# LayerNorm of the convolution: from the compress and prompt stages into the decode passes, with its channel sums added on VectorE

## The reference, cut to what matters

```python
def conformer_conv(u, buf, w, b, ln_g, ln_b):
    xx = jnp.concatenate([buf, u], 1)
    y = dwconv_valid(xx, w) + b
    y = jax.nn.silu(layer_norm(y, ln_g, ln_b))
    return y, xx[:, -(CONV_WIDTH - 1):]

def merge_and_ffn(...):
    c, conv_state = conformer_conv(u, ...)
    x = x + jnp.concatenate([o_nsa, c], -1) @ w_out
    ...
```

## Time and profile before

| what | value |
|---|---|
| median of 3 runs | 1894.15 us (1892.86 to 1899.56) |
| the profiled execution | 1898.77 us, span 1897.0 us |
| mean granted TensorE clock | 0.997 |
| busy share of the span | TensorE 98%, VectorE 66%, ScalarE 20%, GpSimd 6% |
| layer 0: compress, prompt, decode | from about 178, 221 and 308 us of the span |
| layer 0: output projection, layer 1 | from about 452 us; layer 1 follows some 935 us behind layer 0 |

### The profile page before, as it was taken

One profiled execution on the slowest core, in us unless ns is written; L12 is line 12 of the kernel. 1 busy time (PEld: TensorE's weight loads), 2 busy tenths in 40 slices (PEclk: granted clock), 3 DMA queues, 4 the chain that ended last, 5 costly groups with the idle time before them and its releaser, 6 DMA issues.

```text
span 1897.0 us, 26865 instructions
## 1 busy us (share of the span) xinstructions
PE 1855.6 (98%) x10198; PEld 1414.7 (75%) x10198; DVE 1253.0 (66%) x2636; ACT 371.6 (20%) x957; POOL 118.4 (6%) x219
## 2 busy tenths in 40 slices
PE   8999999999999999999999999998999999999999
PEld 7767677777777777777777676776777777777777
DVE  5899896453666766673268998944536667676631
ACT  2013474322100000100001125832221000000000
POOL 1011400010000000000000113000000000000000
PEclk9999999999999999999999999999999999999999
DMA  7303563673121212131241044057531121222211
GB/s 282 127 1 89 157 204 127 205 241 109 63 67 67 89 67 89 58 133 62 85 161 59 1 141 121 2 179 233 168 109 56 67 89 67 89 67 87 93 61 50
DMA packets 110851, 200.28 MB, mean 106 GB/s; under 512 B 13793, under 2 KB 81650, under 8 KB 105730
## 3 DMA queue, kind: packets, MB, share of 16 engines
q1 hardware_dynamic: 105154, 168.17, 26.6%
q0 software_dynamic: 5568, 30.39, 4.6%
HBM read 190.82 MB, written 15.94 MB: 109 GB/s over the span
## 4 chain that ended last, share of the span: by engine, by line
PE 71%; DVE 20%; SPq 5%; issue 2%; ACT 1%; DMA 1%; POOL 0%; DVEq 0%
PE ps L1048 30%; PE ps L1113 15%; DVE catT L1598 7%; PE ps L612 7%; PE ps L599 5%; PE ps L748 4%; SPq L363 2%; PE ps L851 2%; PE ps L814 2%; PE ps L833 2%; SPq L345 1%; PE ps L899 1%; DVE catT L1605 1%; PE ps L984 1%; DVE rC L1604 1%
## 5 line engine op out<-in xcount | busy, mean ns | idle before, releaser
L1598 DVE SCALAR_TENSOR_TENSOR catT<-XC,par,catT 128x512 f32<-128x512 f32 x240 | 180.3, 751 | 7.5
L2097 DVE TENSOR_TENSOR xT<-xT,ps 128x288 f32<-128x288 f32 (+3 forms) x55 | 41.7, 758 | 153.2 <-PE ps L1113 152.9
L1048 PE MATMUL ps<-catT,rD 128*128 128x288 f32 x528 | 131.6, 406 | 0.0
L1048 PEld LDWEIGHTS ps<-catT,rD 128*128 128x128 f32 x528 | 100.3, 190 | 27.7
L1048 PE MATMUL ps<-catT,XC 128*128 128x288 f32 x480 | 119.8, 406 | 0.4 <-DVE rD L2011 0.4
L748 PE MATMUL ps<-WR,rD 128*128 128x254 f32 (+1 forms) x512 | 119.2, 382 | 0.2
L1463 ACT ACTIVATE rD<-rD 128x592 f32<-128x592 f32 x44 | 30.7, 697 | 450.2 <-DVE rD L2039 450.2
L1048 PE MATMUL ps<-rA,WR 128*128 128x288 f32 x448 | 117.8, 406 | 0.0
L1048 PEld LDWEIGHTS ps<-catT,XC 128*128 128x128 f32 x480 | 91.0, 190 | 26.2 <-issue 1.2
L748 PEld LDWEIGHTS ps<-WR,rD 128*128 128x128 f32 x512 | 93.3, 187 | 18.7 <-issue 2.9
L1048 PEld LDWEIGHTS ps<-rA,WR 128*128 128x128 f32 x448 | 85.1, 190 | 23.5
(11 more groups left out here) (371 smaller groups left out, 3341.8 us busy)
## 6 DMA issues: line engine op xcount, KB each, us to landing
WR<-in_w_up SPq DMA_DIRECT2D x56, 512.0 KB, 3.8
WR<-in_kvc SPq DMA_DIRECT2D x128, 128.0 KB, 2.4
rB<-in_ksT SPq DMA_DIRECT2D x256, 64.0 KB
rB<-in_w_up SPq DMA_DIRECT2D x32, 512.0 KB, 4.4
rD<-in_kvc SPq DMA_DIRECT2D x96, 128.0 KB
rD<-in_w_down SPq DMA_DIRECT2D x8, 1408.0 KB, 7.7
rB<-in_w_down SPq DMA_DIRECT2D x6, 1408.0 KB, 6.2
WR<-in_w_glu SPq DMA_DIRECT2D x16, 512.0 KB, 3.7
```

The costliest lines, as they stand in the source:

```text
L1048: ins = mm(ps[:, bank, 0:HN], w[:, k, :], h[:, k, :], start=k == 0, stop=k == 3)
L1598: ins = stt(yc[:, 0:SEQ], xc[:, k:k + SEQ], w, yc[:, 0:SEQ], ALU.mult, ALU.add)
L2097: step(tt(x, x, src, ALU.add))
```

## The change

The sum over channels is split: VectorE adds the four tiles (`ln_add`), then TensorE multiplies one tile of sums by ones (`conv_sum`, 2 matmuls in place of 8), and the same for the squares (`ln_squares`, `conv_sum`). The mean is taken at the prompt's end (`ln_centre`), the squares' sum and variance at p = 0, the inverse root at p = 1 (`root`, `ln_root`), scaling at p = 1 and 2, and the gates of tiles 0 to 2 at p = 2 and of tile 3 at p = 3. `hidden(l, 2, 3, 1)` is redistributed: ten of its steps go to where `means` stood, three and three into the prompt. Two helper tiles `lnu`, `lnv` lie in the convolution's input tile XC, so the load of the next layer's history there (L415) moves to the decode's end.

```diff
@@ -203,9 +203,7 @@
 o += 2 * NT
-lnsq = [rA[:, 576 * i:576 * (i + 1)] for i in range(2)]
-lnmu = rA[:, 1152:1728]
-lnrs = [rA[:, 4192:4192 + HN], rB[:, 5120:5120 + HN]]
+lnu, lnv = [XC[:, 2 * i:2 * i + 2, XS0:XS0 + HN] for i in range(2)]
@@ -411,8 +409,6 @@
         sp.wait_ge(*count("uc_out", 16))
-        if l + 1 < DEPTH:
-            sp.dma_start(XC[:, :, XS0:XW], I["hist"][l + 1].rearrange("p (c n) -> p c n", c=CT)).then_inc(sh["hist_in"], 16)
@@ -442,6 +438,9 @@
                 fetch_new(l, p + 2)
+        sp.wait_ge(sh["conv_done"], CT * (l + 1))
+        if l + 1 < DEPTH:
+            sp.dma_start(XC[:, :, XS0:XW], I["hist"][l + 1].rearrange("p (c n) -> p c n", c=CT)).then_inc(sh["hist_in"], 16)
@@ -656,14 +655,6 @@
-    def means(l):
-        pe.wait_ge(sh["tr_kept"], 10 * l + 10)
-        for c in range(CT):
-            pe.wait_ge(*count("conv_made"))
-            for hf in range(2):
-                ins = mm(ps[:, 2 + hf, 0:HN], ones[:, :], catT[:, CT + c, hf * HN:(hf + 1) * HN], start=c == 0, stop=c == CT - 1)
-        ins.then_inc(sh["mu_made"], 1)
@@ -726,7 +717,7 @@
             for i in range(2):
-                ins = tr(ps[:, (5, 7)[t // 2], (2 * (t % 2) + i) * P:(2 * (t % 2) + i + 1) * P],
+                ins = tr(ps[:, (5, 4)[t // 2], (2 * (t % 2) + i) * P:(2 * (t % 2) + i + 1) * P],
@@ -784,15 +775,19 @@
         keys_second(l, 1, NCP, prompt_pick, CG[0])
-        means(l)
+        hidden(l, 2, 3, 1, js=range(10))
...
         prompt_values()
-        for c in range(CT):
-            square_sum(c, 2, lnsq, CT)
         keys_T(NCS)
+    def conv_sum():
+        pe.wait_ge(*count("u_ready"))
+        for hf in range(2):
+            ins = mm(ps[:, 1 + 2 * hf, 0:HN], ones[:, :], lnu[:, hf, :], start=True, stop=True)
+        ins.then_inc(sh["u_summed"], 1)
@@ -855,12 +850,11 @@
         pe.wait_ge(*count("cs_max"))
-        pe.wait_ge(sh["var_made"], 6 * l + 4)
         scores(0)
+        hidden(l, 2, 3, 1, js=range(10, 13))
+        scores(1)
+        hidden(l, 2, 3, 1, js=range(13, 16))
         pe.wait_ge(sh["cmp_in"], 16 * l + 5)
-        hidden(l, 2, 3, 1, js=range(8), bank=4)
-        scores(1)
-        hidden(l, 2, 3, 1, js=range(8, 16), bank=4)
@@ -872,8 +866,9 @@
             turn(v)
+        pe.wait_ge(*count("masked"))
+        conv_sum()
         weigh(15)
-        pe.wait_ge(*count("masked"))
@@ -890,6 +885,8 @@
             pe.wait_ge(*count("ks_in", 512))
+            if p == 0:
+                pe.wait_ge(*count("u_read", 2))
@@ -966,13 +963,14 @@
                 else:
-                    pe.wait_ge(*count("conv_done", 3))
...
                 pe.wait_ge(*count("st_kept", 2))
+                if p == 0:
+                    conv_sum()
@@ -1006,11 +1004,14 @@
             if more:
+                if p == 0:
+                    pe.wait_ge(*count("u_read", 2))
...
                 else:
+                    pe.wait_ge(*count("conv_done", 3))
@@ -1269,10 +1270,6 @@
-    def ln_square(c):
-        act.wait_ge(*count("mu_taken"))
-        square(c, lnsq, catT[:, CT + c, :])
@@ -1323,17 +1320,12 @@
         copy(KcT[4][HD:P, 32:32 + NCP], ps[HD:P, 6, P:P + NCP]).then_inc(sh["kct_kept"], 1)
-        ln_square(0)
-        ln_square(1)
...
         ins.then_inc(sh["vct_kept"], 1)
-        ln_square(2)
-        ln_square(3)
-        act.wait_ge(*count("sq_summed", 2))
@@ -1366,12 +1358,10 @@
         exps(0)
-        root(lnrs[0])
-        root(lnrs[1])
...
         for i in range(2):
-            copy(CT8[:, 4 * i:4 * i + 4, :], ps[:, (5, 7)[i], :].rearrange("p (k n) -> p k n", n=P)).then_inc(sh["ct_kept"], 1)
+            copy(CT8[:, 4 * i:4 * i + 4, :], ps[:, (5, 4)[i], :].rearrange("p (k n) -> p k n", n=P)).then_inc(sh["ct_kept"], 1)
@@ -1393,17 +1383,17 @@
             act.activation(S[:, 2056:2576], S[:, 2056:2576], ACT.Exp, bias=st[:, 15:16], scale=SCALE, accum_out=st[:, 17:18]).then_inc(sh["w_exped"], 1)
-            if p == 0:
-                act.wait_ge(*count("ln_made", 4))
-            else:
-                act.wait_ge(*count("conv_done"))
-            act.activation(thl, catT[:, CT + p, :], ACT.Tanh, scale=0.5).then_inc(sh["ln_tanh"], 1)
+            if not more:
+                act.wait_ge(*count("conv_done", 3))
+                act.activation(thl, catT[:, CT + p, :], ACT.Tanh, scale=0.5).then_inc(sh["ln_tanh"], 1)
...
                 tanhed(tanh[0], NCS)
+            if p == 1:
+                root(lnv)
@@ -1421,6 +1411,10 @@
                 values_kept(NCS, Vc[ba % 4], 2)
+                if p == 2:
+                    act.wait_ge(*count("ln_made", 4))
+                    for c in range(3):
+                        act.activation((halves(thl), lnu, lnv)[c], halves(catT[:, CT + c, :]), ACT.Tanh, scale=0.5).then_inc(sh["ln_tanh"], 1)
@@ -1685,27 +1679,53 @@
+    def ln_add(l):
+        dve.wait_ge(sh["uc_out"], 16 * (l + 1))
+        y = [halves(catT[:, CT + c, :]) for c in range(CT)]
+        tt(lnu, y[0], y[1], ALU.add)
+        step(tt(lnv, y[2], y[3], ALU.add))
+        tt(lnu, lnu, lnv, ALU.add).then_inc(sh["u_ready"], 1)
+    def ln_summed(bias):
+        dve.wait_ge(*count("u_summed"))
+        for hf in range(2):
+            ts(lnv[:, hf], ps[:, 1 + 2 * hf, 0:HN], 1.0 / CC, bias, ALU.mult, ALU.add).then_inc(sh["u_read"], 1)
+        dve.wait_ge(*count("u_read", 2))
     def ln_centre():
-        dve.wait_ge(*count("mu_made"))
-        step(ts(halves(lnmu), ps[:, 2:4, 0:HN], 1.0 / CC, None, ALU.mult))
+        ln_summed(0.0)
         for c in range(CT):
-            tt(catT[:, CT + c, :], catT[:, CT + c, :], lnmu, ALU.subtract).then_inc(sh["mu_taken"], 1)
+            y = halves(catT[:, CT + c, :])
+            ins = tt(y, y, lnv, ALU.subtract)
+        step(ins)
+    def ln_squares():
+        y = [halves(catT[:, CT + c, :]) for c in range(CT)]
+        tt(lnu, y[0], y[0], ALU.mult)
+        step(tt(lnv, y[1], y[1], ALU.mult))
+        for c in range(2, CT):
+            step(tt(lnu, lnu, lnv, ALU.add))
+            step(tt(lnv, y[c], y[c], ALU.mult))
+        tt(lnu, lnu, lnv, ALU.add).then_inc(sh["u_ready"], 1)
...
     def ln_var():
-        dve.wait_ge(*count("sq_summed", CT))
-        count("sq_made", CT)
-        for hf in range(2):
-            ts(lnrs[hf], ps[:, 2 + hf, 0:HN], 1.0 / CC, EPS, ALU.mult, ALU.add).then_inc(sh["var_made"], 1)
-    def ln_root(hf):
+        ln_summed(EPS)
+        dve.sem_inc(sh["var_made"], 1)
+    def ln_root():
         dve.wait_ge(*count("std_made"))
-        step(dve.reciprocal(lnrs[hf], lnrs[hf]))
+        step(dve.reciprocal(lnv, lnv))
...
         y = catT[:, CT + c, :]
-        tt(y[:, 0:HN], y[:, 0:HN], lnrs[0], ALU.mult)
-        step(tt(y[:, HN:NT], y[:, HN:NT], lnrs[1], ALU.mult))
+        step(tt(halves(y), halves(y), lnv, ALU.mult))
         ts(y, y, PV[:, 16 + 34 * c + 32:16 + 34 * c + 33], PV[:, 16 + 34 * c + 33:16 + 34 * c + 34], ALU.mult, ALU.add).then_inc(sh["ln_made"], 1)
+    def conv_gate(c, th):
+        y = halves(catT[:, CT + c, :])
+        dve.wait_ge(*count("ln_tanh"))
+        step(ts(th, th, 0.5, 0.5, ALU.mult, ALU.add))
+        tt(y, y, th, ALU.mult).then_inc(sh["conv_done"], 1)
@@ -1774,11 +1794,9 @@
         key_norm(NCP)
-        ln_centre()
...
         key_norm(NCS)
-        ln_var()
@@ -1815,7 +1833,7 @@
         weight(0)
-        gelu_in(1, NCS, 0, 4)
+        gelu_in(1, NCS, 0)
@@ -1829,14 +1847,13 @@
             weight(v)
-            if v in (1, 4):
-                ln_root(v // 4)
+            if v == 4:
+                ln_add(l)
...
                 gelu_out(1, NCS, 0)
-            if v in (5, 8, 9, 12):
-                ln_scale((5, 8, 9, 12).index(v))
         count("pt_made", sum(BANKS[t] for g, t in STEPS[13:]))
+        ln_centre()
@@ -1860,10 +1877,11 @@
             ts(sc, sc, s[:, 3:4], None, ALU.mult).then_inc(sh["pc_ready"], 1)
-            y = catT[:, CT + p, :]
-            dve.wait_ge(*count("ln_tanh"))
-            step(ts(thl, thl, 0.5, 0.5, ALU.mult, ALU.add))
-            tt(y, y, thl, ALU.mult).then_inc(sh["conv_done"], 1)
+            if p == 2:
+                ln_scale(2)
+                ln_scale(3)
+            if not more:
+                conv_gate(p, halves(thl))
@@ -1903,6 +1921,10 @@
                 gelu_out(*halves_of[1])
+                if p == 0:
+                    ln_squares()
+                if p == 1:
+                    ln_root()
@@ -1915,6 +1937,14 @@
                 key_norm(NCS)
+                if p == 0:
+                    ln_var()
+                if p == 1:
+                    ln_scale(0)
+                    ln_scale(1)
+                if p == 2:
+                    for c in range(3):
+                        conv_gate(c, (halves(thl), lnu, lnv)[c])
```

(4 more changed lines are left out.)

## The result

The changed kernel took 1912.63 us (median of 4 runs, 1912.19 to 1912.98) against 1896.58 for the kernel before (median of 4 runs, 1892.86 to 1899.56): 1.0086 times as long, 95% interval 1.0066 to 1.0107, **16 us slower**.

What follows compares the result with a forecast made beforehand. It took the changed stages as a mixture, VectorE deciding in stretches while TensorE is fed just in time. Terms -0.2 + 0.73 + 3.1 + 1.2 gave +4.8 a layer, +9.6 on 1894.15: 1903.8, range 1893 to 1912.

Steps and rivals of the forecast that it cites:

- Compress, scores(0) +1.4: Compress: ten MLP steps wait for VectorE, so the prompt's first score block starts 1.4 us later, at 222.3.
- Prompt: -0.36, +0.15, +0.73: Prompt: removed reciprocal less the late `mask(1)` -0.36; `ln_add` for the other reciprocal +0.15; new `conv_sum` less an existing wait +0.73.
- Pass p = 0, +3.1: Decode pass p = 0: TensorE waits 2.05 for VectorE's squares, plus 1.04 of sum; the delay passes on in full.
- absorbed rival: End of p = 1: the wait for keys takes in the p = 0 delay; 1897 to 1899.3, chance 0.20.
- Pass p = 1, nothing: Decode pass p = 1: the reciprocal of about 3.9 and two `ln_scale` are covered by slack, costing nothing.
- Pass p = 2, +1.2: Decode pass p = 2: three gates of 3.66 against 2.40 idle on VectorE make the second key norm 1.2 late.
- The clock: Rival: the clock halves behind the idle stretch before the first score block, +3.5 a layer, 1907.3 or 1910.8; chance 0.25.
- `mask(1)`, forecast +0.56: Prompt's start: `mask(1)` follows VectorE's later `cmp_weight` and comes at 228.35, 0.56 later than before.
- The freed matmuls (faster): Rival: TensorE's total work decides, so 6.4 less a layer gives 12.8 in all, 1881.4; chance 0.07.
- The base: Starting time: 9.6 added to the profiled 1898.77 gives 1908.4, and to the run median 1894.15 gives 1903.8.

Runs made afterwards that it cites:

- fill_c: Changed kernel plus unread matmuls in two idle stretches of compress: 8 before the ten MLP steps, 12 before the last turn of keys; 1910.12 us, ratio 1.0081.
- late_sum: Changed kernel with the sum of squares of pass p = 0 moved behind the weighing's first part on TensorE; 1905.59 us, ratio 1.0064.
- gates_late: Changed kernel with the gates of tiles 1 and 2 in pass p = 2 moved behind the output's last instruction; 1907.82 us, ratio 1.0071.
- fill_all: Changed kernel plus 34 unread matmuls a layer filling all four idle stretches (compress, prompt's first turn, pass p = 0); 1900.59 us, ratio 1.0036.
- small_sums: Kernel before with its two channel sums cut from 8 matmuls to 2 each, 12 fewer a layer; 1907.56 us, ratio 1.0067.
- hybrid: Changed kernel with late sum of squares and late gates, the mean made in compress as in the kernel before, `ln_add` left out; 1893.04 us, ratio 0.9988.
- before_again: Kernel before, unchanged, run again; ratio 1.0001, ten runs from 1891.22 to 1902.96 us.
- after_again: Changed kernel, unchanged, measured and profiled again; 1911.2 us, ratio 1.0085.
- split_steps: Changed kernel with the ten MLP steps in compress cut to three, the other seven behind the values' second layer; 1912.82 us, ratio 1.0102.
- combo: Changed kernel with late sum of squares, MLP steps split three and seven, late gates, and 8 unread matmuls before the three steps; 1894.49 us, ratio 1.0002.
- combo_nofill: Changed kernel with late sum of squares, MLP steps split three and seven, and late gates, without unread matmuls; 1905.23 us, ratio 1.0053.

## Why the prediction was wrong

It said 1903.8 within 1893 to 1912, slower the likeliest; the direction held, 16 us were measured where 9.6 were forecast, and 1912.63 lies just past the range. By its own steps:

- **Compress, scores(0) +1.4: right as a sum of waits, wrong as a time.** Measured +3.0 (223.90). In `fill_c`, where the clock holds, the block starts at 221.70, or 222.1 at the start of the other profiles: the forecast 222.3. The term lacked the ten steps at 1.2 GHz (6.26 for 4.66).
- **Prompt: -0.36, +0.15, +0.73.** The new sum took 1.14 (1.04 forecast). From the first score block to the end of p = 0 the changed kernel took 129.8 for 123.8, 6.0 more: 3.6 is the wait and the slow clock in p = 0 (`late_sum`), 1.2 and 1.1 are the two sums. What the shorter MLP pieces and the removed reciprocal gave back and what the low clock from 222 to 229 and from 239 to 242 took cancel to 0.1; the two were not taken apart. A wait of 2.11 for VectorE ahead of the first turn (0.65 before the change) stands nowhere in the sum; VectorE decides there, 3.0 late since `mask(1)`.
- **Pass p = 0, +3.1: right.** The squares ended at 343.1 with seven instructions of 0.76 each; the wait was 2.11 for 2.05. That it passes on was right too (`late_sum`). Of the absorbed rival only the 0.69 wait for keys of layer 0 is left, which is gone in the changed kernel's profile.
- **Pass p = 1, nothing: right** (36.69 for 36.65 between the ends of p = 0 and 1).
- **Pass p = 2, +1.2: not contradicted.** From the end of p = 1 to that of p = 2 it took 40.38 for 39.65, 0.73 more, with the 0.69 wait for keys gone in the same stretch; moving the gates gave back 0.4 to 0.9 (`gates_late`).
- **The clock: the step that failed.** The sum prices every matmul behind a wait at full clock, and gives the fall a chance of 0.25 apart from it, in one stretch, at 3.5 a layer. It fell in all four stretches of layer 0, three of them shorter than the 3.24 it had seen a fall behind the earlier trace rows, and in all four of layer 1 (three of four in the second profile).
  - *The failed terms, in layer 0:* `mask(1)`, forecast +0.56, came at 230.83, +3.04, with 1.6 of it from the ten steps and 0.95 from the first score block at half clock; pass p = 0, forecast +3.1, had 1.5 more behind its wait. For the stretch that the rival had priced at 3.5 that is 1.0 up to `mask(1)`: right in kind, too dear there, and the loss lay in the others.
  - *Its share.* Against an execution without the wait for keys, the change costs 20: the waits and sums 3.9 in layer 1 (`fill_all`), the clock the other 6.5; layer 0 lost 9.6, which with the same 3.9 leaves 5.7 for the clock. With the second profile of the changed kernel the clock's share is 4.6 in layer 1 and 6.9 in layer 0, whose compress stage began 1.0 later there.
  - *Why it was missed.* The stretches of 2.6 and 2.05 us in compress and p = 0 had been worked out and priced only by their length, the third, ahead of the prompt's first turn, had not been seen. The profile before has no idle stretch between 1.8 and 3.2 us, so nothing in it said that the clock would hold; and behind the one of 3.24, for which the prediction read 0.83, it has 0.50 for three microseconds more (17 to 20).
  - The Trainium skill ("TensorE: Matmul & The Clock Gate", section "Part 1: The HAM clock gate"), which the prediction had cited, says that the throttled clock is the default and that activity releases it. The traces of `small_sums` (less activity, low for 24 us) and `fill_all` (unread activity, clock 0.996 where it was 0.988) agree with it in direction; the falls inside busy stretches (`fill_all` from 217 to 223, `hybrid` from 1145) it does not explain, if activity is read as TensorE's busy share.
- **The freed matmuls (faster): refuted directly.** Removing 12 a layer where they stood made the kernel before 13 us slower.
- **The base.** The sum was made against one execution of 1898.77 that had a wait worth 6.2, and was added to a median; the changed kernel lost that wait in its profile, so the two profiles side by side understate the change by as much. Added to the 1893.2 of `before_again`, the same sum would give 1902.8.

What stays open: whether and why the changed kernel meets the wait for keys more rarely (neither of its two profiles has it, and its first four runs lie within 0.8 us, ten of the kernel before within 12). And what decides over a fall: the same wait in the same order had one in one layer or run and none in another (`after_again`, `gates_late`, `split_steps`), and `cmp_scores` in `hybrid` had one in layer 1 and not in layer 0. The length of the stretch alone does not decide it.

## What to carry to other kernels

Matmuls that fill a wait can be worth more than their own time: before moving them away, ask what the engine does in the gap that is left, and price the work behind the gap at half the clock as well. Read the granted clock behind every idle stretch that a change makes, however short, and judge such an edit by a run with the gap filled by unread work, which separates most of the clock from the waits in one comparison (the filling has a price too). Mind what stands behind a gap: here ten MLP steps of 254 columns had the clock back before `cmp_scores` began, while with three of them and then the 64-column matmuls of `cmp_scores` it was low for 17 us (`split_steps`).

## What was unexpected in the hardware

- The granted clock fell to 1.2 GHz behind idle stretches of 2.11 and 2.58 us, in 15 of the 16 stretches of 2.1 to 3.6 us in two profiles of the changed kernel, and in `small_sums` behind 1.18 and 1.97 with a short sum of 1.21 between them.
- It did not fall behind each: 2.11 in p = 0 of `split_steps` in both layers, 2.59 in compress of layer 1 in `gates_late`, and near the span's start not even behind 3.25 in `combo` and `hybrid`, where it fell behind 3.24 in the profiles of before and after the change.
- It also fell while TensorE was shown busy, in runs of matmuls of 64 columns: 0.50 for six of six busy microseconds in `fill_all` (217 to 223), and from 1145 for 11 us in `hybrid`. Once low behind an idle stretch, it stayed so for 17 us in `split_steps`, nearly all of them busy. A busy share of 100% on TensorE says nothing of its clock.
- Eight missing matmuls of 128 columns (2.05 us) in the gap ahead of such a run cost some 10 us in two layers (`combo` against `combo_nofill`).
